# Two-block layer: in the chunked recurrence, the token rows of every head move to the opposite half of the partitions, and single products alternate with the levels of the inverse

## The reference

```python
def step(s, inp):
    r_t, k_t, v_t, kk_t, a_t, w_t = inp
    sa = jnp.einsum("dbhij,dbhj->dbhi", s, kk_t)
    s = (s * w_t[..., None, :] - sa[..., :, None] * (kk_t * a_t)[..., None, :]
         + v_t[..., :, None] * k_t[..., None, :])
    y = jnp.einsum("dbhij,dbhj->dbhi", s, r_t) if readout else None
    return s, y

return lax.scan(step, state0, xs)
```

## Time and profile before

| what | value |
|---|---|
| median of 3 runs | 2006.18 us (2003.2 to 2009.24) |
| the profiled execution | 2008.59 us, span 2006.8 us |
| PE busy | 94% of the span |
| DVE, ACT, POOL busy | 38%, 24%, 12% |
| granted TensorE clock, mean | 0.976 of full |
| the recurrence | from about 1194 to about 1448 us of the span |

### The profile page before, as it was taken

How to read it: one execution, slowest core, us unless ns; L and a number is a source line. 1 busy time by engine, 2 the same in 40 slices (tenths; PEclk the granted TensorE clock), 3 DMA queues, 4 the chain that set the end, 5 groups by cost and what they waited for, 6 DMA issues and landing times.

```text
span 2006.8 us, 33615 instructions
## 1 busy us (share of the span) xinstructions
PE 1891.1 (94%) x13862; PEld 1003.6 (50%) x13862; DVE 764.0 (38%) x1546; ACT 476.8 (24%) x982; POOL 243.3 (12%) x295
## 2 busy tenths in 40 slices
PE   6999999999999999999899959988898999999997
PEld 2455775444444444434355438888733444444443
DVE  3551441111111100022332347766432888988001
ACT  3022552200000000033211544444322222221001
POOL 1150111000000000012000035465200000000000
PEclk9999799999999999999899979999999999999999
DMA  5421001233432223333311200000021222222222
GB/s 206 168 74 66 30 1 63 97 133 126 147 128 82 84 95 126 105 115 137 118 53 53 69 1 5 5 4 4 15 78 63 74 73 81 75 73 73 84 84 94
DMA packets 43861, 158.63 MB, mean 79 GB/s; under 512 B 5016, under 2 KB 5672, under 8 KB 42712
## 3 DMA queue, kind: packets, MB, share of 16 engines
q1 hardware_dynamic: 37440, 133.19, 19.7%
q10 hardware_dynamic: 6296, 23.58, 3.2%
HBM read 152.01 MB, written 6.31 MB: 79 GB/s over the span
## 4 chain that ended last, share of the span: by engine, by line
PE 88%; DVE 5%; ACT 5%; issue 1%; POOL 1%; DMA 0%; ACTq 0%; DVEq 0%; POOLq 0%
PE psum L330 46%; PE psum L1202 21%; PE psum L1990 2%; PE psum L1994 2%; PE psum L995 2%; PE psum L976 1%; PE psum L589 1%; PE psum L1152 1%; DVE mem L2149 1%; PE psum L963 1%; PE psum L1750 1%; PE psum L632 1%; PE psum L1342 1%; PE psum L2001 1%; DVE mem L2177 1%
## 5 line engine op out<-in xcount | busy, mean ns | idle before, releaser
L330 PE MATMUL psum<-mem 128*128 128x512 f32 (+1 forms) x2272 | 963.0, 582 | 30.3 <-DVE mem L483 15.3
L330 PEld LDWEIGHTS psum<-mem 128*128 128x128 f32 x2272 | 427.4, 190 | 536.4 <-issue 521.3
L1202 PE MATMUL psum<-mem 128*128 128x512 f32 x960 | 421.1, 598 | 4.1 <-DVE mem L2463 2.6
L1202 PEld LDWEIGHTS psum<-mem 128*128 128x128 f32 x960 | 181.7, 191 | 235.7 <-issue 228.0
L2544 DVE SCALAR_TENSOR_TENSOR mem<-mem 128x512 f32<-128x512 f32 x352 | 235.1, 746 | 0.0
L386 POOL TENSOR_TENSOR mem<-mem 128x512 f32<-128x512 f32 x24 | 30.4, 1267 | 1082.4 <-ACT mem L370 1082.0
L1990 PE MATMUL psum<-mem 64*64 64x64 f32 x1920 | 74.5, 222 | 11.7 <-DVE mem L2177 4.4
L1295 ACT ACTIVATE mem<-mem 128x512 f32<-128x512 f32 x22 | 13.9, 630 | 290.7 <-DVE mem L1311 290.7
L1231 DVE SCALAR_TENSOR_TENSOR mem<-psum,mem 128x512 f32 x16 | 12.0, 751 | 179.1 <-PE psum L1202 179.1
L1994 PE MATMUL psum<-mem 64*64 64x64 f32 x1920 | 71.2, 221 | 2.6 <-issue 2.4
L1990 PEld LDWEIGHTS psum<-mem 64*64 64x64 f32 x1920 | 65.0, 136 | 17.3 <-DVE mem L2177 10.0
(11 more groups left out here) (341 smaller groups left out, 1758.8 us busy)
## 6 DMA issues: line engine op xcount, KB each, us to landing
mem<-in_units SPq DMA_DIRECT2D x248, 512.0 KB, 3.4
mem<-in_cw ACTq DMA_DIRECT2D x2, 2048.0 KB, 10.3
mem<-in_wn ACTq DMA_DIRECT2D x1, 2048.0 KB, 8.7
bias_tiles<-bias_scratch ACTq DMA_DIRECT2D x1, 2048.0 KB
mem<-bias_tiles ACTq DMA_DIRECT2D x1, 2048.0 KB, 10.3
mem<-in_xT ACTq DMA_DIRECT2D x1, 2048.0 KB, 9.6
x_scratch<-mem ACTq DMA_DIRECT2D x1, 2048.0 KB, 8.7
mem<-x_scratch ACTq DMA_DIRECT2D x1, 2048.0 KB, 7.8
```

The costliest lines, as they stand in the source:

```text
L330: last = pe.matmul(dst, ring[:, slot, k, :], rhs(k), start=(k == 0), stop=(k == 7))
L1202: last = eng.matmul(ps[m % 4], ring[:, slot, k - 8 * part, :], rhs(k), start=(k == 0), stop=(k == ktiles - 1))
```

## The change

Tokens of every head now lie in the half opposite to its channels (`tok(b)` gives `1 - b`). So what goes from tokens to tokens or from channels to channels stays on the diagonal, and every product between channels and tokens is on (0,1) and (1,0) alone. `level` can take a second, single product and issues one matmul of each in turn: `x` with level 0, `raw_beta` with level 2 (before, after level 4), `raw_kappa` with level 4 (before, after level 5), `turn_v` with level 7 (before, after level 6). The double products stay groups of their own: `y` after level 2 as before, `state` after level 4, `turn_bk` after level 8. Level results of a direction lie in one bank (0 or 1), the others in banks 2 to 7. On VectorE `move` goes from ahead of `grow(5)` to ahead of `grow(9)`. The number of matmuls and their sizes stay.

```diff
             E_, O_ = [(0, 0), (1, 0)], [(0, 1), (1, 1)]
             X_ = U_ = Y_ = [(2, 0), (2, 1)]
-            YM_ = [(3, 2), (3, 3)]
-            V_ = S_ = G_ = [(3, 0), (3, 1)]
-            BETA = [(2, 0), (2, 2)]
-            KAPPA = BK = [(3, 0), (3, 2)]
+            S_ = [(2, 2), (2, 3)]
+            YM_ = [(6, 2), (6, 3)]
+            V_ = G_ = [(6, 0), (6, 1)]
+            BETA = [(4, 0), (4, 2)]
+            KAPPA = BK = [(6, 0), (6, 2)]
...
-            def tok(hp, b):
-
-                return ch(1 - b if hp in FLIP else b)
+            def tok(b):
+
+                return ch(1 - b)
...
             def dst(at, hp, r, lo=0, width=C, per=C):
 
-                pair, slot = at
+                bank, slot = at
+                if bank < 2:
+                    lo += slot * 2 * P + hp * C
+                    return psum[r, bank, lo:lo + width]
                 lo += slot * P + (hp % 2) * per
-                return psum[r, 2 * pair + hp // 2, lo:lo + width]
+                return psum[r, bank + hp // 2, lo:lo + width]
...
+                def level(n, d, it, beside=(), done=None):
...
+                    a, b_ = (g[:, :, 1], T) if n % 2 == 0 else (Tt, Z) if n < 9 else (Z, Tt)
+                    at = O_[d] if n % 2 else E_[d]
+                    for i in range(2):
+                        for hp in (i, i + 2):
+                            for b in range(2):
+                                t = tok(b)
+                                own = eng.matmul(dst(at, hp, t), a[t, hp, :], b_[t, hp, :], start=True, stop=True)
+                                for f in beside[:1]:
+                                    other = f(hp, ch(b), t)
+                        for f in beside[1:]:
+                            for hp in (i, i + 2):
+                                for b in range(2):
+                                    other = f(hp, ch(b), tok(b))
+                    own.then_inc(q["made"], 1)
+                    if beside and d:
+                        other.then_inc(both[done], 1)
+
+                def both_of(products, it, done):
+                    for d in range(2):
+                        last = each(*products(d, it))
+                    last.then_inc(both[done], 1)
...
+                def state(d, it):
                     eng.wait_ge(both["u_kept"], it + 1)
-                    eng.wait_ge(both["fresh_kept"], it + 1)
+                    eng.wait_ge(both["moved"], 2 * it + 2)
...
+                        eng.wait_ge(both["y_kept"], it - 3)
...
+                def raw_beta(d, it):
                     if it:
-                        eng.wait_ge(both["moved"], 2 * it + 2)
-                    raw(KAPPA, kd, it, "kappa")
-
-                def turn_v(it):
+                        eng.wait_ge(both["beta_masked"], it)
+                    return raw(BETA, kka, d, it)
+
+                def raw_kappa(d, it):
+                    if it:
+                        eng.wait_ge(both["fresh_kept"], it)
+                    if lat(it - 1):
+                        eng.wait_ge(both["ym_kept"], it - 4)
+                    return raw(KAPPA, kd, d, it)
...
-                        level(n, 0, it)
-                        level(n, 1, it)
-                        if n == 0 and it:
-                            x(it - 1)
-                        elif n == 1 and it:
+                        for d in range(2):
+                            if n == 0 and it:
+                                level(n, d, it, x(d, it - 1), "fed")
+                            elif n == 2 and it < LAST:
+                                level(n, d, it, raw_beta(d, it + 1), "beta")
+                            elif n == 4:
+                                level(n, d, it, raw_kappa(d, it), "kappa")
+                            elif n == 7:
+                                level(n, d, it, turn_v(d, it), "turned")
+                            else:
+                                level(n, d, it)
+                        if n == 1 and it:
                             if lat(it - 1):
                                 ym(it - 1)
                             u(it - 1)
                         elif n == 2 and lat(it - 1):
-                            y(it - 1)
-                        elif n == 3 and it:
-                            state(it - 1)
-                        elif n == 4 and it < LAST:
-                            raw_beta(it + 1)
-                        elif n == 5:
-                            raw_kappa(it)
-                        elif n == 6:
-                            turn_v(it)
-                        elif n == 7:
-                            turn_bk(it)
+                            both_of(y, it - 1, "y")
+                        elif n == 4 and it:
+                            both_of(state, it - 1, "s")
+                        elif n == 8:
+                            both_of(turn_bk, it, "turned")
                         elif n == 9:
                             fresh(it)
...
                 def mask_beta(it):
                     eng.wait_ge(both["beta"], it + 1)
+                    if lat(it - 2):
+                        eng.wait_ge(both["y"], it - 5)
                     mask(BETA, "g1", 0, it, "beta_masked")
...
                     for n in (1, 3, 5, 7, 9):
-                        if n == 5:
+                        if n == 5 and it < LAST:
+                            mask_beta(it + 1)
+                        elif n == 7:
+                            mask_kappa(it)
+                        elif n == 9:
                             if it:
                                 move(it - 1)
                             if it < LAST:
-                                mask_beta(it + 1)
-                        elif n == 7:
-                            mask_kappa(it)
-                        elif n == 9 and it < LAST:
-                            begin(0, it + 1)
-                            begin(1, it + 1)
+                                begin(0, it + 1)
+                                begin(1, it + 1)
                         grow(n, 0, it)
```

More of the change, by code:

```diff
@@ L1974, in each @@
                                 for b in range(2):
[L1975 removed]
+                                    last = f(hp, ch(b), tok(b))
                     return last
[L1978 removed]
+                def level(n, d, it, beside=(), done=None):
                     s, q = st_[d], e[d]
@@ L2033, in ym, with y @@
                     last.then_inc(both["ym"], 1)
[L2035 removed]
+                def y(d, it):
                     eng.wait_ge(both["u_kept"], it + 1)
[L2037 to L2044 removed]
@@ L2057, in state @@
-                    last.then_inc(both["s"], 1)
-                def raw(k, left, it, done):
-                    for d in range(2):
-                        w, a, r = left[d], alpha(d, it), rho[d][it % 3]
-                        eng.wait_ge(e[d]["laid"], it + 1)
-                        if lat(it):
-                            last = each(lambda hp, c, t: eng.matmul(dst(k[d], hp, t, 0, 2 * C, 2 * C), w[c, chunk(d, it), hp, :],
-                                                                    view(r[c, hp, :], 0, [[a.offset - r.offset, 2], [1, C]]),
-                                                                    start=True, stop=True))
-                        else:
-                            last = each(lambda hp, c, t: eng.matmul(dst(k[d], hp, t, C, C, 2 * C), w[c, chunk(d, it), hp, :],
-                                                                    a[c, hp, :], start=True, stop=True))
-                    last.then_inc(both[done], 1)
@@ L2072, in raw_beta @@
-                def raw_beta(it):
-                    if lat(it - 2):
-                        eng.wait_ge(both["y_kept"], it - 5)
-                    elif it >= 2:
-                        eng.wait_ge(both["u_kept"], it - 1)
-                    raw(BETA, kka, it, "beta")
-                def raw_kappa(it):
-                    if it:
-                        eng.wait_ge(both["moved"], 2 * it + 2)
-                    raw(KAPPA, kd, it, "kappa")
-                def turn_v(it):
-                    eng.wait_ge(both["kappa_masked"], it + 1)
-                    for d in range(2):
-                        n = chunk(d, it)
-                        last = each(lambda hp, c, t: eng.matmul(dst(V_[d], hp, t), vC[c, n, hp, :], ident[c, c], start=True,
-                                                                stop=True))
-                    last.then_inc(both["turned"], 1)
@@ L2092, in turn_bk @@
-                def turn_bk(it):
-                    eng.wait_ge(both["turns_kept"], 2 * it + 1)
-                    for d in range(2):
-                        n = chunk(d, it)
-                        last = each(lambda hp, c, t: eng.matmul(dst(BK[d], hp, t, 0, C, 2 * C), kka[d][c, n, hp, :],
-                                                                ident[c, c], start=True, stop=True),
```

(14 more changed lines are left out.)

87 lines of the change are left out of this document (46 added, 41 removed).

## The result

The changed kernel takes 2028.27 us, the median of 4 runs (2027.38 to 2029.22); the kernel before, on the same chip, 2004.69 (2000.74 to 2009.24). The ratio is 1.0115, with a 95% interval of 1.0099 to 1.013: slower, by 23.6 us. The profiled execution took 2029.22 us, with a span of 2027.4, which is 20.6 more than before's.

A forecast was written before the change was run, and what follows sets the result against it. PE, busy for 94% of the span, was taken as the bound. Late iterations 16.5, iteration 4 1.8, the last 4.1 and iterations 1 to 3 4.2 sum to 26.6, taken as 26; with 2006.2 that gives 2032 us, range 2018 to 2042.

The forecast's parts named there:

- the sum: Recurrence, all iterations walked by stretches: 26.6 us more, taken as 26.
- Pace by the fullest quarter: TensorE: a quarter takes a 64-column record in 58 ns whatever others do; a group's time is its fullest quarter's.
- The rival: Not slower: TensorE starts groups early on idle quarters, giving back up to 28.8 us; same 0.04, faster 0.03.
- The quarters' count: Lower bound by quarters alone: 31 double groups 0.93 us longer each, 28.8; 13.8 saved; net 15.0 us more.
- Cover lost: Groups no longer filling PE's waits in the recurrence: what lies between 15 and 26 us.
- The halves of single products: `x`, `turn_v` and narrow raw products: 13.8 us saved in the count by quarters, at 0.46 us a group.
- The late iterations: A late iteration takes 23.9 us in place of 21.2; six (5 to 10) give 16.5 us more.
- the walk: Stretch-by-stretch costing of one late iteration between level starts: 23.9 us after the change, 21.2 before.
- the small loss: Rival: less cover lost, or issue gaps fall into the new waits; 10 to 18 us more, about 2021; chance 0.14.
- The other terms: Iterations 1 to 3 4.2 us more, iteration 4 1.8, the last 4.1, iteration 0 nothing.
- `move` late: Rival: VectorE's `move` delays `begin` and level 9, up to 1.5 us in 11 iterations; 34 to 50 more; chance 0.09.
- The bank: One bank per direction's level: costed at nothing; rival that halves exclude one another, 112 us more, 2144, chance 0.02.

The follow-up runs named there:

- 8: Kernel before, with only the double products `y`, `state` and `turn_bk` put on two quarters, order unchanged: 2012.43 us, ratio 1.0051.
- 7: Changed kernel with `state` moved back behind level 3, nothing else moved: 2018.88 us, ratio 1.0084.
- 11: Changed kernel with `state` behind level 3, and `turn_v` in banks 4 and 5, waiting for `mask_beta`, beside level 6: 2010.86 us, ratio 1.0051.
- 12: The kernel of 11 with `turn_bk` also moved back, behind level 7 in place of level 8: 2016.33 us, ratio 1.0055.
- 4: Changed kernel with single products issued as whole groups behind both directions of their level, nothing alternating: 2044.55 us, ratio 1.0214.
- 1: Kernel before with its own order; only token rows of pairs 0 and 1 moved, so channel-token products use two quarters: 2027.34 us, ratio 1.0132.
- 2: Changed kernel with the double products `y`, `state` and `turn_bk` over four quarters again: 2018.48 us, ratio 1.0076.
- 5: Changed kernel with double products beside levels too: `y` with level 3, `state` with 5, `turn_bk` with 8: 2011.83 us, ratio 1.0049.
- 6: The kernel of 5 with `turn_v` in the banks of `raw_beta` and beside level 6 in place of level 7: 2010.28 us, ratio 1.0041.
- experiment 9: Changed kernel with `state` behind level 3, `turn_bk` behind level 7, `turn_v` beside level 6, both masks ahead of `grow(5)`: 2021.43 us, ratio 1.0097.

## Why the prediction was right, and where its sum was not

- **Direction and size.** 2032 was predicted, in 2018 to 2042, and 2028.3 measured. The stage grew by 21.4 us where the sum had 26.6. (One stretch of the sum, level 5 to 7 in iterations 1 to 3, adds 2.45 and 0.85 to 3.4; they are 3.3, which is 0.3 us in all.)
- **Pace by the fullest quarter: right.** `y` takes 1.81 us from its first to its last record (1350.49 to 1352.30), level and `x` together 0.93. What the sum missed is the seam: from the start of `y` to that of level 3 it is 1.65, since level 3 starts 0.17 early. The rival had allowed for a lead of two records; it is 6, too little for its 29.
- **What a double product costs.** The quarters' count gave 31 times 0.93, 28.8. Measured alone (8) it is 9.7: seams take a part that the count put at nothing, and 5.6 us fill waits and issue gaps of the kernel before.
- **Cover lost: right in kind.** `state` alone (7) was worth up to 7.0 us, and with `turn_v` and `turn_bk` also back (11, 12) 12.8. Of these, 4.9 came with `turn_v` freed from the mask, for which it waits before the change as well, so they are not all cover that the change lost. The steps of 4 put places and order together at 18.2. So that a double group in the wrong place costs is shown; how much of the 21.4 is cover depends on the order in which the steps are taken.
- **The halves of single products.** By the stages of 1 and 8 they cost 12.7 (282.4 less 269.7), where the count had 13.8 for them, and alternating gives 19.2 back, more than that. The new places take the rest.
- **The late iterations: the term that was mis-sized.** The sum has "A late iteration thus takes 23.9 us in place of 21.2: 2.8 more. Six have all of it". From `fresh` to `fresh` the six took 23.8, 24.4, 23.6, 24.7, 24.2 and 23.6, on the mean 24.03. That the walk's 23.9 meets this mean is in part luck, as the iteration that it walks took 23.55: the seams make it shorter than the sum, and others have issue gaps. And before, the six took 22.8, 22.4, 21.2, 22.5, 22.2 and 22.4, on the mean 22.25, where the walk had used the one that was shortest. So six give 10.7 and not 16.5; that is the whole difference to the sum. Of the 1.06 between mean and shortest, 0.3 are issue gaps (1.19 an iteration against 0.88 in the one walked; 0.22 are left after the change) and 0.3 waits for the transpose; the rest lies in no gap above 0.15 us, and its cause is open. The earlier trace rows had shown an iteration of 22.8, and the prediction put that under the small loss instead of into the base.
- **The other terms.** Iterations 1 to 3 took 1.0, 1.6 and 2.0 more (4.2 predicted, 4.6 measured), iteration 4 1.9 (1.8), the rest, with the last and the tail, 4.2 (4.1). In iteration 3, a fall of the clock takes part (below).
- **`move` late: it did not happen.** It starts at 1363.65, `grow(9)` at 1366.64, and `fresh` waits for ScalarE's copy of `turn_bk` (L2299), not for VectorE.
- **The bank: no cost.** All 8 matmuls of a direction's level write one bank now, and a level keeps 29 ns a record and 226 ns on the mean. The rule of the Trainium skill, "TensorEngine Tiling (Array Packing)", Restrictions and Gotchas, that different row tiles cannot access one PSUM bank simultaneously, does not show where their output halves differ.

## What to carry to other kernels

Count a group of small matmuls by its fullest quarter of the array, and then ask what its time covers. Here the halves alone cost 22.4 us, and the new places and order cost nearly as much again, mostly because groups no longer stood in a gap that PE has to wait through anyway; alternating gave 19.2 back. A count by quarters gives neither of the last two. Take the base of a walk as the mean over all iterations, not from the shortest one. And where several products share an array, short groups (16 records) on idle quarters behind one another come within 5 us of alternating one by one, groups of 32 lose 19; so look at the place of a group in the chain before its fine order.

## What the runs showed that was not expected

**Issue gaps go with the pace.** A gap in which PE waited for nothing that the profile shows takes 9.3 us before, 3.7 after, 0.2 where everything runs on two quarters (1), 13.4 where double products run on four quarters (2), 17.9 and 21.7 where they and the levels fill four quarters together (5, 6). The kernel before moves hardly anything in this stage but its instructions. Its DMA from 1190 to 1450:

```profile
q8 instruction: 66, 1.08, 1.8%
```

That is 66 packets of 16 KB, while PE has 16768 records, matmuls and weight loads: one packet for each 254. In the window from 1341 to 1347, in 40 slices of 0.15 us, one such packet begins, at 1343.4:

```profile
GB/s 0 0 0 0 0 0 0 0 0 0 0 0 0 0 0 0 109 0 0 0 0 0 0 0 0 0 0 0 0 0 0 0 0 0 0 0 0 0 0 0
```

The gap of 0.88 us in the earlier trace rows ends at 1346.20, 2.8 us later. It is so with all of them. Each of the 18 issue gaps before ends 2.29 to 2.90 us behind the start of such a packet, each of the 9 after 2.29 to 2.80, and over the fourteen traces of this case all 176 lie between 2.15 and 2.94. Packets are at least 3.2 us and mostly near 4 us apart, so a moment taken at random would fall there about one time in five; of PE's 660 other waits, 141 do. With 127 matmul records (half of 254) to a packet, a packet each 3.2 us gives an estimate of 25 ns a matmul record for the fastest supply seen: slower than the 14.5 ns of four quarters, faster than the 29 of two. It fits that PE used up its instructions faster than they came. No run changed the supply of instructions, so the cause is argued from this coincidence and not shown by an experiment.

**The clock can fall behind short waits.** In the changed kernel, in windows of 2 us, PE is busy for 0.96 of 2.00 us at full clock, and after it runs at half, 1.2 GHz, for a while:

```profile
1262.00:1264.00 2.00, 1.72 (x65) 1.63 (x60) 0.19 (x1) 1.17 (x5) 1.65 (x3) 1.00 0.03 8
1264.00:1266.00 2.00, 0.96 (x25) 0.82 (x24) 0.99 (x3) 0.00 (x0) 1.92 (x4) 1.00 0.03 8
1266.00:1268.00 2.00, 1.87 (x47) 1.73 (x50) 1.45 (x6) 0.44 (x2) 1.87 (x3) 0.70 0.00 0
1268.00:1270.00 2.00, 1.80 (x64) 1.62 (x60) 1.16 (x3) 0.61 (x3) 0.00 (x0) 0.50 0.00 0
```

Ahead of it were an issue gap of 0.78 us and a wait of 0.55. The shares of 0.30 and 0.50 are 1.6 us, a part of the 2.0 us of iteration 3. The kernel before has 1.00 there. That waits of 1.4 us can cost as much again in clock is also what experiment 9 had. But four other waits of that length there had no fall behind them, nor had an issue gap of 1.66 us in 5, and why is open.
